# Feed-forward weights split by column halves, right after their half's matmuls instead of between the residuals

## The reference

```python
def swiglu(h, w_gate, w_up, w_down):
    return (jax.nn.silu(h @ w_gate) * (h @ w_up)) @ w_down

xs = xs + g_f * swiglu(modulate(xs, norm_ffn_g[l], sh_f, sc_f), w_gate[l], w_up[l], w_down[l])
```

## Time and profile before

| | us |
|---|---|
| median of 3 runs | 1957.2 (1952.45 to 1959.02) |
| the profiled execution, device time | 1961.39 |
| its span, first to last instruction | 1959.6 |
| PE busy | 1746.5 (89%) |
| DVE busy | 1177.4 (60%) |
| ACT busy | 719.4 (37%) |
| mean granted PE clock | 0.957 of full speed |

### The profile page before, as it was taken

The page is one execution under the profiler, slowest core; times in us unless marked ns, Lnnn a source line. Parts: engine busy times, 40 slices in busy tenths (PEclk is TensorE's granted clock), DMA queues, the critical chain, the costliest instruction groups (busy, mean ns, idle before and its releaser), DMA issues.

```text
span 1959.6 us, 29154 instructions
## 1 busy us (share of the span) xinstructions
PE 1746.5 (89%) x11708; PEld 1671.6 (85%) x11708; DVE 1177.4 (60%) x2221; ACT 719.4 (37%) x1377; POOL 223.6 (11%) x242
## 2 busy tenths in 40 slices
PE   4699778888899999999989967888889999999997
PEld 3699667778899999999989966777889999999997
DVE  6998676783676667676552167678454434444334
ACT  2423665672521221122143266567343121211222
POOL 0001524330000000000010052523000000000001
PEclk9999798999899999999989979899989999999998
DMA  9474000004234433433122010000312222112201
GB/s 317 141 230 125 24 1 2 1 23 150 87 121 161 148 107 119 158 120 118 40 71 78 28 39 1 1 2 23 116 58 65 65 86 64 64 64 91 80 21 54
DMA packets 107912, 159.82 MB, mean 82 GB/s; under 512 B 4976, under 2 KB 85680, under 8 KB 107568
## 3 DMA queue, kind: packets, MB, share of 16 engines
q1 hardware_dynamic: 105024, 152.52, 23.4%
q0 software_dynamic: 640, 2.92, 0.5%
q10 hardware_dynamic: 2160, 3.23, 0.5%
HBM read 155.08 MB, written 3.57 MB: 81 GB/s over the span
## 4 chain that ended last, share of the span: by engine, by line
PE 65%; DVE 25%; ACT 6%; issue 3%; POOL 1%; ACTq 1%; POOLq 0%; DVEq 0%
PE ps L584 21%; PE ps L585 20%; PE ps L586 20%; DVE ps L1228 5%; DVE x L1292 5%; DVE gw L1213 4%; DVE pT L1213 2%; DVE negmax L1430 1%; PE ps L791 1%; DVE K L1213 1%; PE ps L648 1%; DVE Q L1324 1%; PE ps L592 1%; DVE V L1213 1%; ACT pT L1118 1%
## 5 line engine op out<-in xcount | busy, mean ns | idle before, releaser
L584 PE MATMUL ps<-hT,gw 128*128 128x320 f32 x1408 | 437.0, 310 | 6.8 <-DVE hT L1213 6.8
L585 PE MATMUL ps<-hT,gw 128*128 128x320 f32 x1408 | 436.5, 310 | 0.0
L586 PE MATMUL ps<-hT,gw 128*128 128x320 f32 x1408 | 436.5, 310 | 0.0
L1292 DVE SCALAR_TENSOR_TENSOR x<-ps,mod,x 128x320 f32<-128x320 f32 (+2 forms) x576 | 207.7, 430 | 135.9 <-PE ps L586 135.6
L584 PEld LDWEIGHTS ps<-hT,gw 128*128 128x128 f32 x1408 | 265.8, 189 | 7.3 <-issue 7.3
L585 PEld LDWEIGHTS ps<-hT,gw 128*128 128x128 f32 x1408 | 265.8, 189 | 0.0
L586 PEld LDWEIGHTS ps<-hT,gw 128*128 128x128 f32 x1408 | 265.6, 189 | 0.0
L1514 DVE TENSOR_TENSOR mm<-sl,ps 128x320 f32<-128x320 f32 x88 | 42.7, 487 | 342.6 <-issue 210.2
L584 PE MATMUL ps<-act,dw 128*128 128x320 f32 x704 | 219.7, 312 | 17.1 <-DVE x L1292 16.7
L585 PE MATMUL ps<-act,dw 128*128 128x320 f32 x704 | 217.5, 309 | 0.0
L586 PE MATMUL ps<-act,dw 128*128 128x320 f32 x704 | 217.5, 309 | 0.0
(11 more groups left out here) (199 smaller groups left out, 3718.6 us busy)
## 6 DMA issues: line engine op xcount, KB each, us to landing
gw_raw<-in_w_gate SPq DMA_DIRECT2D x22, 1024.0 KB, 5.4
gw_raw<-in_w_up SPq DMA_DIRECT2D x22, 1024.0 KB, 8.0
dw_raw<-in_w_down SPq DMA_DIRECT2D x22, 1024.0 KB, 4.9
ada_w<-in_w_adaT SPq DMA_DIRECT2D x42, 512.0 KB, 6.2
ada_wf<-in_w_adaT SPq DMA_DIRECT2D x34, 512.0 KB, 7.4
wi_raw<-in_w_in SPq DMA_DIRECT2D x16, 912.0 KB, 5.6
ada_wq<-in_w_adaT SPq DMA_DIRECT2D x20, 512.0 KB, 4.0
wo_raw<-in_w_out SPq DMA_DIRECT2D x16, 512.0 KB, 4.3
```

The costliest lines, as they stand in the source:

```text
L584: pe.matmul(dst, lh, rh, start=start, stop=False, skip_group_check=True)
L585: pe.matmul(dst, lh, rl, start=False, stop=False, skip_group_check=True)
L586: return pe.matmul(dst, ll, rh, start=False, stop=stop, skip_group_check=True)
L1292: i = ve.scalar_tensor_tensor(out=x[:, o, c0:c1], in0=ps[:, banks + hf_, s0:s0 + c1 - c0], scalar=mod[:, l, part * KD + o, q:q + 1], in1=x ...
```

## The change

Each of the two splits (ACT's copy, DVE's subtraction) of gate and up becomes two, one for each column half: 128 x 8 x 128 elements instead of 128 x 2048. The half j of the next block is split after block b's half j is done: on ACT right after its two roundings of half j, on DVE right after the low parts of `act` (and, for j = 0, after the down weights). Between the residuals nothing is left. The semaphores count halves, so their values double; PE now waits for a weight half ahead of each of the four groups (w, j), where it waited for whole tiles ahead of j = 0. In the first block of a layer the splits stay where they were, cut in two.

The core of the diff:

```diff
                 for b in range(1, FB):
-                    sp.wait_ge(gate_ready, l * FB + b)
-                    sp.wait_ge(up_ready, l * FB + b)
+                    sp.wait_ge(gate_ready, 2 * (l * FB + b))
+                    sp.wait_ge(up_ready, 2 * (l * FB + b))
...
-                            if j == 0:
-                                pe.wait_ge(up_ready if w else gate_ready, l * FB + b + 1)
+                            pe.wait_ge(up_ready if w else gate_ready, 2 * (l * FB + b) + j + 1)
...
+                def gw_split(b, j):
+
+                    cols = slice(j * P, (j + 1) * P)
                     for w in range(2):
-                        sc.activation(gw[:, w, 0], gw_raw[:, w], ACT.Copy).then_inc(gw_hi, 1)
+                        sc.activation(gw[:, w, 0, :, cols], gw_raw[:, w, :, cols], ACT.Copy).then_inc(gw_hi, 1)
...
-                    if not last:
-                        sc.wait_ge(gu_ps, base * 2 + 8)
-                        gw_split(b + 1)
+                        if not last:
+                            if j == 0:
+                                sc.wait_ge(gw_in, 32 * (l * FB + b) + 64)
+                            sc.wait_ge(gu_ps, base * 2 + 4 * j + 4)
+                            gw_split(b + 1, j)
...
                         if j == 0:
                             down_lo(b)
+                        if not last:
+                            gate_lo(b + 1, j)
+                            up_lo(b + 1, j)
                     for o in range(KD):
-                        if o == 2 and not last:
-                            gate_lo(b + 1)
-                        if o == 3 and not last:
-                            up_lo(b + 1)
                         residual(l, l * XD + KD + b * KD + o + 1, o, 2 * (o % 4), 5)
```

More of the change, by code:

```diff
@@ L506, in _ @@
                 else:
-                    sp.wait_ge(gate_ready, l * FB)
-                    sp.wait_ge(up_ready, l * FB)
+                    sp.wait_ge(gate_ready, 2 * l * FB)
+                    sp.wait_ge(up_ready, 2 * l * FB)
                     wi_load(l, 0)
@@ L864, in first_gate_up @@
                     pe.wait_ge(x_done, l * XD + 1 + KD)
-                    pe.wait_ge(gate_ready, l * FB + 1)
-                    pe.wait_ge(up_ready, l * FB + 1)
+                    pe.wait_ge(gate_ready, 2 * l * FB + 2)
+                    pe.wait_ge(up_ready, 2 * l * FB + 1)
                     for k in range(KD):
@@ L873, in first_gate_up @@
                                     m.then_inc(gu_ps, 1)
-                    settled(pe, passed_pe)
+                    pe.wait_ge(up_ready, 2 * l * FB + 2)
                     for hf_ in range(2):
@@ L1164, in _ @@
                         square(2 * l + 1, l * XD + 2, o - 3)
-                def gw_split(b):
-                    sc.wait_ge(gw_in, 32 * (l * FB + b) + 32)
+                def gw_split(b, j):
+                    cols = slice(j * P, (j + 1) * P)
                     for w in range(2):
-                        sc.activation(gw[:, w, 0], gw_raw[:, w], ACT.Copy).then_inc(gw_hi, 1)
-                gw_split(0)
+                        sc.activation(gw[:, w, 0, :, cols], gw_raw[:, w, :, cols], ACT.Copy).then_inc(gw_hi, 1)
+                sc.wait_ge(gw_in, 32 * l * FB + 32)
+                gw_split(0, 0)
+                gw_split(0, 1)
                 for k in range(5, KD):
@@ L1485, in _, with gate_lo, up_lo @@
                         add_square(l, o - 3)
[L1487 to L1493, removed]
+                def gate_lo(b, j):
+                    cols = slice(j * P, (j + 1) * P)
+                    ve.wait_ge(gw_hi, 4 * (l * FB + b) + 2 * j + 1)
+                    lo(gw[:, 0, 1, :, cols], gw_raw[:, 0, :, cols], gw[:, 0, 0, :, cols]).then_inc(gate_ready, 1)
+                def up_lo(b, j):
+                    cols = slice(j * P, (j + 1) * P)
+                    ve.wait_ge(gw_hi, 4 * (l * FB + b) + 2 * j + 2)
+                    lo(gw[:, 1, 1, :, cols], gw_raw[:, 1, :, cols], gw[:, 1, 0, :, cols]).then_inc(up_ready, 1)
                 def down_lo(b):
@@ L1497, in down_lo @@
                     lo(dw[:, 1], dw_raw[:], dw[:, 0]).then_inc(dw_ready, 1)
-                gate_lo(0)
+                gate_lo(0, 0)
+                gate_lo(0, 1)
                 add_square(l, 5)
@@ L1501, in _ @@
                 add_square(l, 6)
-                up_lo(0)
+                up_lo(0, 0)
+                up_lo(0, 1)
                 inverse(2 * l + 1)
```

## The result

Beside the kernel before, the change ran in 1937.5 us in the median (1936.1 to 1939.6, 4 runs), the kernel before in 1956.2 us: a ratio of 0.9906, 95% interval 0.9887 to 0.9926, so 18.7 us less. Measured again beside the kernel before, it was 0.9927 (0.9912 to 0.9942), 14.3 us less. The forecast was 1940.0 us and a gain of 17.2 us. The profiled execution of the changed kernel has a span of 1937.8 us. Two executions among the experiments, 2039.8 us in experiment 1 and 2586.9 us in experiment 3, ran at a lower granted clock (0.83 and 0.62) and are left out of the medians and ratios given there.

What follows compares the result with a forecast made beforehand. PE was taken to bound the kernel, pausing 1.10 us in each of 20 blocks for a late residual. -22.0 + 2.3 + 2.5 = -17.2 us gave 1940.0 us for the median, range 1931 to 1951.

Steps and rivals of the forecast that it cites:

- What goes: Down phase, tile 7: PE's 20 pauses of 1.10 us waiting for residual 3 all go, 22.0 us.
- Cost of halves: Middle blocks: strided halves cost as flat ones, 1.222 us on DVE and 1.056 on ACT; two take 2.28 and 1.96.
- The bound of twice the price: Strided halves on DVE and ACT: upper bound of 2 times flat, from short strided rows; 1 times was taken.
- Covers: Middle blocks: idle time hides the halves, 2.26 us on DVE for j = 0 and 2.83 before the first residual; cost 0.
- The slack of 1.2 us: Start of the down phase: residual 0 ends at 645.7, PE wants it for tile 4 at 647.0.
- First block of layer 0: No idle time on DVE there: two halves push PE's wait for act from 0.39 to 2.7 us, costing 2.3 once.
- The clock's part: Behind the lengthened pause in layer 0's first block, the granted clock falls: 2.5 us taken, ends 0 and 4.9.
- rival A: Layer 0's first block: the clock stays up, so the 2.5 us fall away: 1937.5 us; chance 0.33.
- The sum: Whole kernel: -22.0 + 2.3 + 2.5 = -17.2 us, median 1940.0 us.
- B: Middle blocks: dear strided halves delay residual 0, PE waits ahead of tile 4; at twice flat 1984 us; chance 0.07.
- C: Layer 0's blocks: DVE's queue with its dot products slips, paying back that layer's 11 us: 1951 us; chance 0.06.
- D: Each block: the pause only moves, something unseen costs PE 1.1 us: 1962 us, or 1957; chance 0.09.

Runs made afterwards that it cites:

- experiment 1: Changed kernel with the half splits put back where the kernel before has them, so split without move: 1963.8 us, ratio 1.0046; second run 1961.5 us, 1.0036.
- experiment 3: Changed kernel with half j = 1's two low parts put back ahead of residuals 2 and 3: 1936.2 us, ratio 0.9893.
- experiment 2: Kernel before with its two whole low parts moved ahead of residual 0, uncut: 1967.0 us, ratio 1.0064.
- experiments 4 and 5: Changed kernel with half j = 1's gate low part taken twice on DVE: 1936.0 us, ratio 0.9913; taken three times: 1962.4 us, 1.0040.
- experiment 7: Changed kernel with one dot product of half j = 1 in layer 0's first block moved behind the residuals: 1932.8 us, ratio 0.9898.
- experiment 6: Changed kernel with four dot products of layer 0's first block moved behind its residuals: 1930.3 us, ratio 0.9870; second run 1932.0 us, 0.9889.

## Why the prediction was right, point by point

- **What goes.** 22.0 us forecast for the 20 pauses. Layer 1, where nothing was added, gave 10.9 us of its 11.0, and a middle block takes 42.23 us as forecast (42.24). Shown by the profile; experiments 1 to 3 show that it was DVE's queue ahead of residual 3, and by experiment 3 half of it would have been enough to clear.
- **Cost of halves.** 1.22 and 1.06 us forecast, 1.221 and 1.044 measured; two halves 2.36 us on DVE from first start to last end, holding up what stands behind them by 2.27 (629.76 to 632.03 in the block above; 2.28 forecast), and 1.99 on ACT (1.96). The bound of twice the price, taken from short strided rows with an outlier, was far off the truth.
- **Covers.** Half j = 0 in DVE's idle 2.26 us: mm began without idle time and no later than before, at no cost. Half j = 1: residuals from 644.55, as forecast (644.6). The slack of 1.2 us stood up to experiments 4 and 5 (the prediction's own 647.0 and 645.7 give 1.3).
- **First block of layer 0.** 2.28 us more forecast; the pause grew by 2.27. The clock's part was forecast at 2.5 us. Experiment 7 puts it at 2.9 us; experiment 6, which frees both, at 5.7 - 2.66 = 3.0. So the choice of the dense stretch of the earlier trace rows as the nearest case was right, and rival A (no fall of the clock) is out, though its 1937.5 us is what the median came to. The profile shows the fall that A denies, so that agreement is chance.
- **The sum.** -17.2 forecast; -16.9 in the feed-forward parts. The timed 18.7 us (14.5 to 22.1 by the interval) and the 14.3 us of the second measurement lie on either side and are no finer test than that.
- **Rivals.** B needs halves 1.35 times as dear, and they are not; C and D are excluded by the 42.23 us of a layer 0 block and by layer 1's 466.4 us. The split adds work to DVE: its gw pieces are busy for 103.8 us, the whole ones were for 100.3. Experiment 1 shows that this costs where it isn't hidden: 24.8 us of waits in place of 22.0, so 2.8 us for the 40 splits, where the prediction's 0.16 us each came to 6.4. In the change idle time covers it. The Trainium skill (VectorE: DVE Perf Modes, section on the TRN2 errata) says that each such instruction pays a fixed latency, so that small tiles pay it more often. The trace agrees in kind, with 0.07 us for each further piece of experiment 1.

## What to carry to other kernels

When an engine off the critical path releases buffers for the one on it, count its work between two deadlines, not its share of the span: 4.4 us ahead of residual 3 cost 1.1 us in each block, 2.3 us cost nothing. Cut such work so that each piece fits an idle stretch that the trace shows, and check the one iteration in which that stretch is missing: here the first block cost 5 us of a gain of 22, and moving four instructions brought it back.

## What the runs showed of the hardware

- After a pause of 1.51 us in a dense stretch PE's granted clock stayed at 1.00; after 2.66 us, with the same matmuls before and behind it, it fell to 0.50 for 6.0 us, at a price of about 3 us, more than the pause itself. In experiment 2's profile a pause of 2.58 us in the same block, ahead of down tile 4, was followed by a mean of 0.72 over 556 to 562 us. No feed-forward part of these runs has a pause between 1.51 and 2.58 us, so where it turns stays open; the 1.80 us pause of the earlier trace rows, which is 1.76 in PE's own row and lies in a less dense stretch (PE busy for 8.09 of the 10 us from 286 to 296, in the profile of before), was followed by 0.51.
- Outside the feed-forward parts, executions of one and the same kernel differ by several us: the stretch between the two feed-forward parts took 454.4 us in the first profile of experiment 6's kernel and 459.1 in the second; it was 461.1 in the profile of before and 459.8 in that of the change.
